# Expert rows gathered from token order and outputs scattered to token order through index lists made on chip, in place of sorted copies in DRAM

## The chip, the cores and the metric

One core of a Trainium2 chip runs the whole program. The metric is device time in microseconds (us); lower is better. TensorE is PE, VectorE is DVE, ScalarE is ACT, GpSimd is POOL and SyncE is SP. Everything is float32.

## The reference, cut to what matters

Two transformer blocks run one after the other on 512 tokens of 1024 features. The first has four recurrent mixers, a layer norm, a top-4-of-32 mixture of experts and a gated embedding; the second has two layers of retention, pooling and attention. The change touches the experts only:

```
logits = x2d @ router_w + router_b
top_val, top_idx = top_k(logits, 4);  gate = softmax(top_val)
# the 2048 assignments are sorted by expert into blocks of rows of one expert
hg, hl = split(xblk @ w_gu[e] + b_gu[e]);  hg = min(hg, 7);  hl = clip(hl, -7, 7)
y = (hg * sigmoid(1.702 * hg) * (hl + 1)) @ w_down[e] + b_down[e]
ffn[token] = sum over its four assignments of gate * y
```

## The kernel before, in words

**Stages.** The input projection with the four mixers fills the first 470 us, then come the output projection, the norm and the router (to about 549 us), then the experts (to about 1639 us), the sum over the four assignments with the gated embedding (to about 1700 us), and the second block.

**Blocks.** The 2048 assignments are laid out in blocks of 96 slots (3 groups of 32 lanes), each block of one expert, at most 56 blocks; slots that an expert does not fill stay empty. With these inputs the loop turns 32 times, one block for each expert, so on average 64 of the 96 slots hold a token. `dest` (L2993) is the slot of each assignment: 96 x block + 32 x group + lane.

**The sorted copies.** `x_sorted` and `y_sorted` are DRAM arrays with one row of 4 KB for each of the 5376 slots. SP fills both with zeros at the start (L1849 to L1858, 44 MB, in six transfers between the first weight pieces), and only then loads the masks into the place that the zeros came from (L1861). After the router, POOL scatters each token's row four times into `x_sorted` (L1959, 16 indirect transfers of 128 rows, 8 MB). ACT reads the rows of a block in four transfers of 32 partitions by 3 groups by 1 KB (`from_sorted`, L637 to L641), each slot's row being four quarters of 1 KB, and writes the outputs of a block in four more (L2265 to L2267). After the loop POOL gathers from `y_sorted` the four outputs of each token (L1967, 16 indirect transfers).

**One turn of the loop.** Every engine runs the same loop and meets the others at semaphores; `Turn` (L285) makes the values out of the turn's number. PE (L1376): gate_up(1), (2), (3), which are three quarters of this block's first product, then gate_up(0) and the bias of the next block, then the down product. A weight piece is 2 MB; a block takes six, kept in six ring slots that SP refills as PE frees them (L1901 to L1915). DVE (L3029): finds the next block's expert, waits for the next block's rows (`rows_landed`, L3056), transposes half of them aside, waits until PE is done with gate_up(1), transposes the other half into `xg` (L3059, counted in `rows_turned`), and only then adds the bias and clips for this block's groups (L3035 to L3038), which is what PE's next gate_up(0) waits for (`gu_drained`). ACT: at `rows_turned` it issues the load of the rows two blocks on, then the sigmoids, the bias copy, the three copies of the outputs out of PSUM (L2263), and their store.

**Around the loop.** The first block's rows do not come from DRAM: PE picks them out of SBUF with a one-hot product (L1351). The second block's rows are the first load (L2244); ACT waits for all 16 scatters before it (L2243). After the loop ACT waits for all stores, raises `all_stored`, and POOL gathers; DVE adds the weighted outputs tile by tile (L3075), in between normalizes the meta tokens, and PE follows with the gated embedding.

## Time and profile before

| | us |
|---|---|
| Median of 3 runs (3220.64 to 3222.08) | 3221.12 |
| The profiled execution's own time | 3224.01 |
| Its span, first to last instruction | 3221.9 |
| PE busy | 3060.8 (95%) |
| DVE busy | 1206.7 (37%) |
| ACT busy | 557.6 (17%) |
| POOL busy | 49.0 (2%) |
| Bytes moved by DMA | 743.71 MB |

The table is of one profiled execution. A busy PE is one that has matmuls in flight. The parts of the page and the answers of the trace say of each idle stretch what ended it, and of each transfer how long it took from its issue until it landed. The granted clock is PE's, as a share of full speed.

### The profile page before, as it was taken

To read this page: it belongs to the slowest core of one execution; us is meant where nothing else is said; L and a number is where in the kernel's file an instruction comes from. 1 tells how busy PE (TensorE), PEld (TensorE's weight loads), DVE (VectorE), ACT (ScalarE), POOL (GpSimd) and SP (SyncE) were. 2 spreads that over 40 slices of the span, in tenths; PEclk is the share of its full clock that TensorE was granted. 3 is DMA by queue.
4 is the path that set the end of the run, shared out by engine and by line. 5 is a ranking of instruction groups with operands and counts; after the bars stand their busy time and mean duration, and the time that the engine had idled before them with its cause. 6 is when DMAs were issued, how large, how long until landed. Compare 5 with 4: busy or idle time off the path is not lost.

```text
span 3221.9 us, 52861 instructions
## 1 busy us (share of the span) xinstructions
PE 3060.8 (95%) x22497; PEld 1727.1 (54%) x22497; DVE 1206.7 (37%) x2398; ACT 557.6 (17%) x1138; POOL 49.0 (2%) x58
## 2 busy tenths in 40 slices
PE   9878889799999999999989999999999999999999
PEld 3355555243334333333434767675686748775866
DVE  1633365223222232323256443335425362335231
ACT  1332321011111111111112131131101411131000
POOL 0000001000000000000020000000000000000000
PEclk9888969899999999999989999999999999999999
DMA  9900115899999999999972333243434344242542
GB/s 400 362 1 27 53 38 213 327 406 411 406 408 404 404 409 404 410 405 413 402 275 94 135 111 145 104 177 131 165 129 158 135 176 151 105 177 105 196 164 97
DMA packets 100924, 743.71 MB, mean 231 GB/s; under 512 B 11512, under 2 KB 38720, under 8 KB 57936
## 3 DMA queue, kind: packets, MB, share of 16 engines
q1 hardware_dynamic: 62224, 687.49, 53.8%
q10 hardware_dynamic: 32624, 30.52, 2.9%
q0 software_dynamic: 5968, 24.14, 1.9%
q8 instruction: 82, 1.34, 0.2%
q14 instruction: 26, 0.21, 0.0%
HBM read 674.98 MB, written 67.13 MB: 230 GB/s over the span
## 4 chain that ended last, share of the span: by engine, by line
PE 51%; DMA 29%; DVE 5%; issue 2%; ACTq 1%; ACT 1%; POOL 1%; DVEq 0%; SPq 0%
DMA arena<-x_sorted 28%; PE psum L1727 20%; PE psum L1704 11%; PE psum L1661 3%; PE psum L1650 3%; PE psum L899 1%; ACTq L641 1%; PE psum L1452 1%; PE psum L917 1%; PE psum L1293 1%; PE psum L1768 1%; PE psum L1416 1%; PE psum L1508 1%; DMA x_sorted<-arena 1%; PE psum L1554 1%
## 5 line engine op out<-in xcount | busy, mean ns | idle before, releaser
L1341 PE MATMUL psum<-weight_ring,arena 128*32 128x512 f32 x6192 | 676.0, 594 | 42.2 <-DVE arena L3035 41.5
L1727 PE MATMUL psum<-arena,weight_ring 128*128 128x256 f32 (+1 forms) x2816 | 638.5, 385 | 2.8 <-ACT arena L2380 2.8
L1727 PEld LDWEIGHTS psum<-arena,weight_ring 128*128 128x128 f32 x2816 | 530.0, 190 | 101.2 <-issue 12.9
L1341 PEld LDWEIGHTS psum<-weight_ring,arena 128*32 128x32 f32 x6192 | 199.9, 110 | 498.7 <-issue 455.8
L1416 PE MATMUL psum<-weight_ring,arena 128*32 128x256 f32 x6144 | 338.2, 380 | 0.0
L1416 PEld LDWEIGHTS psum<-weight_ring,arena 128*32 128x32 f32 x6144 | 196.7, 110 | 152.9 <-issue 26.8
L3057 DVE STREAM_TRANSPOSE arena<-arena 128x384 f32<-128x384 f32 x32 | 18.6, 580 | 643.1 <-DMA arena<-x_sorted 643.1
L1704 PE MATMUL psum<-weight_ring 128*128 128x512 f32 x468 | 204.1, 593 | 4.9 <-DMA weight_ring<-down 3.7
L1704 PE MATMUL psum<-weight_ring,arena 128*128 128x512 f32 x470 | 204.4, 593 | 0.7 <-ACT arena L2380 0.7
L3414 DVE TENSOR_TENSOR weight_ring<-weight_ring,psum 128x256 f32<-128x256 f32 (+1 forms) x88 | 37.4, 425 | 432.9 <-PE psum L1727 431.3
L3314 DVE TENSOR_TENSOR weight_ring<-weight_ring 128x1024 f32<-128x1024 f32 (+1 forms) x140 | 157.2, 1172 | 8.6 <-PE psum L1704 7.8
L1704 PEld LDWEIGHTS psum<-weight_ring 128*128 128x128 f32 x468 | 88.5, 190 | 116.0 <-issue 108.8
L1704 PEld LDWEIGHTS psum<-weight_ring,arena 128*128 128x128 f32 x470 | 89.0, 190 | 111.7 <-issue 109.9
L915 PE MATMUL psum<-arena,weight_ring 128*128 128x512 f32 x288 | 134.0, 616 | 11.1 <-DMA weight_ring<-weights 6.8
L2440 ACT ACTIVATE weight_ring<-psum 128x256 f32<-128x256 f32 (+1 forms) x88 | 34.1, 387 | 586.5 <-PE psum L1727 586.3
L1661 PE MATMUL psum<-arena,weight_ring 128*128 128x272 f32 (+1 forms) x512 | 116.8, 386 | 0.0
L2257 ACT ACT_TABLE_LOAD x32 | 41.1, 1283 | 417.0 <-issue 417.0
L1661 PEld LDWEIGHTS psum<-arena,weight_ring 128*128 128x128 f32 x512 | 96.1, 189 | 19.9 <-issue 2.8
L915 PEld LDWEIGHTS psum<-arena,weight_ring 128*128 128x128 f32 x288 | 54.6, 196 | 76.7 <-issue 67.3
L917 PE MATMUL psum<-weight_ring,arena 128*128 128x512 f32 (+1 forms) x192 | 90.9, 601 | 0.0
L2263 ACT COPY arena<-psum 128x256 f32<-128x256 f32 x96 | 36.0, 375 | 293.2 <-PE psum L1416 286.7
L1650 PE MATMUL psum<-weight_ring,arena 128*128 128x262 f32 (+2 forms) x320 | 86.2, 426 | 0.0
(446 smaller groups left out, 2716.3 us busy)
## 6 DMA issues: line engine op xcount, KB each, us to landing
weight_ring<-exp_gu SPq DMA_DIRECT2D x129, 2048.0 KB, 11.4
weight_ring<-weights SPq DMA_DIRECT2D x80, 2048.0 KB, 7.8
weight_ring<-exp_down SPq DMA_DIRECT2D x64, 2048.0 KB, 10.8
weight_ring<-down SPq DMA_DIRECT2D x48, 1024.0 KB, 6.1
x_sorted<-arena SPq DMA_DIRECT2D x2, 10752.0 KB
arena<-x_sorted ACTq DMA_DIRECT2D x132, 96.0 KB, 21.0
y_sorted<-arena ACTq DMA_DIRECT2D x128, 96.0 KB, 16.8
y_sorted<-arena SPq DMA_DIRECT2D x2, 5632.0 KB, 39.4
```

Source lines behind the costliest of these rows:

```text
L915: mm = pe.matmul(bank, w[:, k, a:a + P], x_t[:, k, :], start=(k == 0), stop=(k == KT - 1))
L917: mm = pe.matmul(bank[:, 0:width], x_t[:, k, t * P:(t + 1) * P], w[:, k, a:a + width], start=(k == 0), stop=(k == KT - 1))
L1341: mm = pe.matmul(psum[j * GROUP:(j + 1) * GROUP, g, :], xg[:, k // 4, g, k % 4 * GROUP:(k % 4 + 1) * GROUP], w[:, kk, j * 512:(j + 1) * 51 ...
L1416: mm = pe.matmul(psum[j * GROUP:(j + 1) * GROUP, 3 + g, 0:256], hid_t[:, g, k * GROUP:(k + 1) * GROUP], w[:, kk, j * 256:(j + 1) * 256], s ...
L1650: mm = pe.matmul(bank[:, 0:width], h2_t[:, k, OFF[t]:OFF[t] + P], w[:, k, 0:width], start=first, stop=last)
L1661: mm = pe.matmul(bank[:, 0:b - a], w[:, k, c:c + P], h2_t[:, k, a:b], start=first, stop=last)
L1704: mm = pe.matmul(bank, left[stationary][:, q, :], right[part][f][half][:, n, :], start=(q == 0 and name not in ADDED_TO), stop=(q == pairs ...
L1727: mm = pe.matmul(bank[:, 0:b - a], w[:, k, col:col + P], h2_t[:, k, a:b], start=(k == 0), stop=(k == KT - 1))
L2257: T.did(act.activation(sig[:, g, :], swi[:, g, 0:256], ACT.Sigmoid, scale=SWIGLU_ALPHA), swish_given)
L2263: T.did(act.copy(y_out[:, g, :], psum[:, 3 + g, 0:256]), y_drained)
L3314: V.did(dve.tensor_tensor(b[out[0]][out[1]], b[one[0]][one[1]], b[other[0]][other[1]], op), right_ready)
L3414: V.did(dve.tensor_tensor(g, g, bank[:, 0:b - a], ALU.mult), main.drained["v"])
```

## The change

The sorted copies go. `token_rows` holds the 512 normalized rows in token order, as 2048 quarters of 1 KB; `y_tokens` holds an output for each assignment, at row (choice, token, quarter). Every block's load becomes three indirect transfers on POOL's queue, one for each group, whose 128 partitions are 4 quarters by 32 lanes; every store becomes three indirect transfers likewise. The row numbers come from two lists, `idx_x` and `idx_y` (128 partitions by 168 group slots). They come out of a product: for each of the 16 (tile, choice) pairs a one-hot of the lane times the number of the assignment, against a one-hot of the group slot (64 matmuls of 128 x 32 against 128 x 168), and ten DVE instructions on the sum. A slot without a token gets a number beyond the bound, and the transfer is told to pass over such numbers. The zeros at the start go, the masks and the weight pieces are loaded without them, and the loads after the loop become four direct ones of 2 MB on SP's queue.

```diff
-CONST3 = Layout(before=P, iota=P, split=SPLITS, lane=1)
+SLOT_UNITS = NB * GROUPS
+UNIT_PARTS = (5, 11)
+STEP = 1024
+NOWHERE = 65536
+CONST3 = Layout(before=P, iota=SLOT_UNITS, split=SPLITS, lane=1, ids=TT * TOP, quarter=1)
...
-        x_sorted = nc.dram_tensor("x_sorted", (SORTED, D), F32, kind="Internal").ap()
-        y_sorted = nc.dram_tensor("y_sorted", (SORTED, D), F32, kind="Internal").ap()
+        token_rows = nc.dram_tensor("token_rows", (SEQ * 4, 256), F32, kind="Internal").ap()
+        y_tokens = nc.dram_tensor("y_tokens", (SEQ * TOP * 4, 256), F32, kind="Internal").ap()
...
                 gate_up(0, first_used)
+                pe.wait_ge(sem("first_rows_ready"), 2)
+                for n in range(TT * TOP):
+                    units = one_u[0][:, n, :] if n < UNIT_PARTS[0] else one_u[1][:, n - UNIT_PARTS[0], :]
+                    for j in range(4):
+                        mm = pe.matmul(psum[j * GROUP:(j + 1) * GROUP, SLOT_BANK, 0:SLOT_UNITS], one_r[:, n, :], units, start=(n == 0),
+                                       stop=(n == TT * TOP - 1), skip_group_check=True)
+                mm.then_inc(sem("rows_picked"), 1)
                 pe.wait_ge(rows_turned, 2)
...
-            sp.wait_ge(sem("zeros_ready"), 1)
-            store_zeros(x_rows, 0, SORTED // P // 2, sem("rows_stored"))
-            load_piece(2)
...
-            sp.wait_ge(sem("rows_stored"), 32)
-            sp.wait_ge(y_stored, 64)
             sp.dma_start(c1[:, P:P + D], io["const1"][:, P:P + D]).then_inc(sem("masks_landed"), 16)
-            for n in range(5, 9):
+            for n in range(2, 9):
                 load_piece(n)
...
             sp.wait_ge(sem("all_stored"), 1)
+            load_given(0)
             load_piece2(1, io["ple_gate"][1])
+            load_given(1)
+            load_given(2)
+            sp.wait_ge(sem("ffn_ready"), 1)
+            load_given(3)
...
         def _(pool):
-            pool.memset(zero_row, 0.0).then_inc(sem("zeros_ready"), 1)
-            pool.wait_ge(sem("rows_stored"), 32)
             for t in range(TT):
                 pool.wait_ge(sem("x1_ready"), t + 1)
                 pool.tensor_copy(x1_by_tile[:, t], x1[:, t, :].rearrange("p (q k j) -> p k q j", q=4, k=KT)
                                  ).then_inc(sem("x1_by_tile_ready"), 1)
-            pool.wait_ge(sem("dest_ready"), 1)
...
+                pool.dma_start(token_rows[t * P * 4:(t + 1) * P * 4, :].rearrange("(p q) d -> p (q d)", q=4), x1[:, t, :]
+                               ).then_inc(y_stored, 16)
+
+            def gather_rows(index):
+                for g in range(GROUPS):
+                    pool.indirect_dma_start(rows_in[:, g, :], None, token_rows, bass.IndirectOffsetOnAxis(ap=index[:, g:g + 1], axis=0),
+                                            bounds_check=SEQ * 4 - 1, oob_is_err=False).then_inc(rows_landed, 16)
+
+            pool.wait_ge(y_stored, 16 * TT)
+            pool.wait_ge(sem("rows_listed"), 1)
+            gather_rows(idx_x[:, GROUPS:2 * GROUPS])
...
+            with pool.Fori(0, blocks) as i:
+                T = Turn(pool, i, own, per, credit, sem("expert_pool_passed"))
+                T.wait(rows_turned, 1)
+                T.hold()
+                T.did(pool.tensor_copy(now_x, idx_x[:, bass.ds((i + 2) * GROUPS, GROUPS)]))
+                T.settle()
+                T.hold()
+                gather_rows(now_x)
+                T.wait(y_drained, GROUPS)
+                T.hold()
+                T.did(pool.tensor_copy(now_y, idx_y[:, bass.ds(i * GROUPS, GROUPS)]))
+                T.settle()
+                T.hold()
+                for g in range(GROUPS):
+                    pool.indirect_dma_start(y_tokens, bass.IndirectOffsetOnAxis(ap=now_y[:, g:g + 1], axis=0), y_out[:, g, :], None,
+                                            bounds_check=SEQ * TOP * 4 - 1, oob_is_err=False).then_inc(y_stored, 16)
+            pool.wait_ge(y_stored, blocks * BLOCK_DONE + 16 * TT)
+            pool.sem_inc(sem("all_stored"), 1)
...
-                act.wait_ge(sem("scattered"), 16 * TT * TOP)
-                from_sorted(act, slice(ROWS_B, 2 * ROWS_B), rows_landed)
...
-                    T.wait(rows_turned, 1)
-                    from_sorted(act, bass.ds((i + 2) * ROWS_B, ROWS_B), rows_landed)
...
-                    T.wait(y_drained, GROUPS)
-                    for j in range(4):
-                        dst = y_sorted[bass.ds(i * ROWS_B, ROWS_B), j * 256:(j + 1) * 256].rearrange("(g r) n -> r g n", g=GROUPS)
-                        act.dma_start(dst, y_out[j * GROUP:(j + 1) * GROUP, :, :]).then_inc(y_stored, 16)
...
-                V.did(dve.tensor_copy(dest, dest_f), sem("dest_ready"))
+                then(dve.tensor_copy(dest, dest_f))
+                V.did(dve.tensor_scalar(lane_i, dest, GROUP - 1, None, ALU.bitwise_and))
+                then(dve.tensor_scalar(unit_i, dest, 5, None, ALU.logical_shift_right))
+                V.did(dve.tensor_copy(lane_f, lane_i))
+                then(dve.tensor_copy(unit_f, unit_i))
...
+                then(dve.tensor_tensor(one_r, each_of(iota[:, 0:GROUP], pairs), along(lane_f, GROUP), ALU.is_equal))
+                V.did(dve.tensor_tensor(one_r, one_r, along(CONST3(c3, "ids"), GROUP), ALU.mult))
+                for part, at in enumerate((0, UNIT_PARTS[0])):
+                    of = unit_f[:, at:at + UNIT_PARTS[part]]
+                    V.did(dve.tensor_tensor(one_u[part], each_of(iota, UNIT_PARTS[part]), along(of, SLOT_UNITS), ALU.is_equal))
+                V.settle()
+                V.did(dve.memset(den, 0.0), sem("first_rows_ready"))
...
+                dve.wait_ge(sem("rows_picked"), 3)
...
+                then(dve.tensor_scalar(empty, token, 0.0, float(NOWHERE), ALU.is_equal, ALU.mult))
...
+                V.did(dve.tensor_copy(idx_x, empty))
...
+                V.did(dve.tensor_copy(idx_y, token), sem("rows_listed"))
```

## Rows read from the trace of the kernel before

**Rows 1.** Page, part 4: the chain that ended last, by line.

```profile
DMA arena<-x_sorted 28%; PE psum L1727 20%; PE psum L1704 11%; PE psum L1661 3%; PE psum L1650 3%; PE psum L899 1%; ACTq L641 1%; PE psum L1452 1%; PE psum L917 1%; PE psum L1293 1%; PE psum L1768 1%; PE psum L1416 1%; PE psum L1508 1%; DMA x_sorted<-arena 1%; PE psum L1554 1%
```

**Rows 2.** Windows: stretch, length, busy by engine, granted clock, DMA share, GB/s.

```profile
549.00:604.00 55.00, 29.96 (x255) 14.03 (x258) 10.10 (x23) 1.58 (x3) 17.03 (x16) 0.78 0.83 327
...
611.90:1627.90 1016.00, 998.22 (x12156) 387.24 (x12160) 283.34 (x776) 129.39 (x248) 0.00 (x0) 1.00 1.00 402
```

**Rows 3.** Waits in the loop: total us, times, longest.

```profile
DVE arena L3057 <- DMA arena<-x_sorted: 605.0, 30, 22.9
...
PE psum L1341 <- DVE arena L3035: 17.8, 15, 1.7
```

**Rows 4.** PE's timeline: start, length, work; first, two middle, last down product.

```profile
611.81 10.57 PE L1416 MATMUL psum<-weight_ring,arena 128*32 128x256 f32 x192
...
1004.26 10.57 PE L1416 MATMUL psum<-weight_ring,arena 128*32 128x256 f32 x192
1014.65 20.78 PE L1341 MATMUL psum<-weight_ring,arena 128*32 128x512 f32 x192
...
1036.35 10.57 PE L1416 MATMUL psum<-weight_ring,arena 128*32 128x256 f32 x192
...
1627.82 10.57 PE L1416 MATMUL psum<-weight_ring,arena 128*32 128x256 f32 x192
```

**Rows 5.** DMA queues, 612 to 1628 us: packets, MB, share of 16 engines.

```profile
q1 hardware_dynamic: 26359, 383.85, 93.0%
q10 hardware_dynamic: 27776, 24.40, 7.4%
```

**Rows 6.** Row loads: landing time in the loop, and for the first load.

```profile
DMA to landing us min/median/max: 2.2/21.8/31.7
...
arena<-x_sorted ACTq DMA_DIRECT2D x4, 96.0 KB, 2.4
```

**Rows 7.** PE's timeline between the router and the first down product.

```profile
545.91 10.65 PE L1351 MATMUL psum<-arena 128*128 128x96 f32 x64 [1.32 <-issue]
556.50 5.36 PE L1341 MATMUL psum<-weight_ring,arena 128*32 128x512 f32 x48
...
564.23 15.66 PE L1341 MATMUL psum<-weight_ring,arena 128*32 128x512 f32 x144 [0.71 <-issue]
...
603.61 7.27 PE L1341 MATMUL psum<-weight_ring,arena 128*32 128x512 f32 x48 [23.73 <-DVE arena L3035]
```

**Rows 8.** DVE's timeline in the same stretch.

```profile
547.62 0.69 DVE L2991 TENSOR_TENSOR arena<-arena 128x512 f32<-128x512 f32 x1
...
549.07 0.17 DVE L2993 CAST arena<-arena 128x16 int32<-128x16 f32 x1
...
549.22 2.01 DVE L2996 TENSOR_TENSOR arena<-arena 128x1792 f32<-128x1792 f32 x1
...
601.94 0.58 DVE L3057 STREAM_TRANSPOSE arena<-arena 128x384 f32<-128x384 f32 x1 [38.13 <-DMA arena<-x_sorted]
```

**Rows 9.** The chain over the wait for the 16 scatters.

```profile
570.20 27.86 DMA x_sorted<-arena
```

**Rows 10.** POOL: an indirect issue in the timeline; its copies' group, mean ns.

```profile
552.56 0.99 POOL L1959 DMA_INDIRECT x_sorted<-arena  x1 [0.30 <-issue]
...
L1953 POOL COPY arena<-arena 128x1024 f32<-128x1024 f32 x4 | 4.2, 1062 | 530.8 <-DVE arena L2937 530.8
```

**Rows 11.** Waits of PE in the first 200 us: total us, times, longest.

```profile
PE psum L915 <- DMA weight_ring<-weights: 6.8, 2, 6.2
```

**Rows 12.** After the loop: timelines of ACT, DVE, POOL; one SP issue.

```profile
1639.00 2.93 ACTq L2267 DMA_DIRECT2D y_sorted<-arena  x4
...
1656.71 3.93 DVE L3075 SCALAR_TENSOR_TENSOR arena<-weight_ring,arena 128x1024 f32<-128x1024 f32 x3 [3.08 <-DMA weight_ring<-y_sorted,arena]
...
1666.03 2.88 POOL L1967 DMA_INDIRECT weight_ring<-y_sorted,arena  x1 [0.30 <-issue]
...
weight_ring<-ple_gate SPq DMA_DIRECT2D x1, 2048.0 KB, 8.6
```

83 lines of the change are left out of this document (42 added, 41 removed).

## The prediction

> **What bounds the kernel now.** I read the chain that ended last first: its largest line, 28% of the span, is the transfer of block rows out of `x_sorted` [rows 1]. The windows say where that is: from the first to the last down product (1016 us) PE is busy for 998 us at the full granted clock, while the DMA engines are busy all the time at 402 GB/s; in the 55 us before, PE is busy for only 30 us [rows 2]. The waits then separate the two: DVE stands 605 us for block rows, but that costs PE only 17.8 us, in 15 turns, where the next gate_up finds its PSUM bank not drained [rows 3]. PE's timeline gives the floor: where nothing waits, a turn is 1036.35 - 1004.26 = 32.09 us of matmuls back to back, and the 31 turns between the first and the last down product took 1627.82 - 611.81 = 1016.0 us, or 32.77 us each [rows 4]. So the loop is held by PE, with 1016.0 - 31 x 32.09 = 21.2 us on top that come from late rows.
>
> Why are they late? The queue of the weights (q1) and that of row loads and stores (q10) carried almost the same number of packets, 26359 and 27776, but 383.85 against 24.40 MB [rows 5]. Four row transfers land 2.4 us after their issue when alone, but 21.8 us (median) and up to 31.7 us in the loop [rows 6]. I read this as turns taken between the queues: a 1 KB packet waits for a 16 KB one. Per turn of the loop the engines spend 0.930 x 1016 / 31 = 30.5 us on weights and 0.074 x 1016 / 31 = 2.4 us on rows, 32.9 us in all. They are as full as PE is.
>
> **The change, part by part.**
>
> *Zeros, 44 MB, gone.* They share the queue with the weight pieces, but in the first 200 us PE waits for weights only 6.8 us, of which 6.2 us are the very first pieces, ahead of any zero [rows 11]. What hides the zeros is that a piece is asked for one piece ahead of its use. Nothing gained; nothing can be lost, since queue and SP only get emptier. The masks land earlier than before, for users that did not wait. Price 0.
>
> *Scatters gone, start of the loop.* Now POOL scatters 16 times, the chain stands 27.86 us behind the last of them [rows 9], DVE gets the second block's rows at 601.94 us [rows 8], and PE resumes at 603.61 us after an idle time of 23.73 us [rows 7]. After the change:
> - DVE builds one-hots behind `dest` (549.07 us): two of 512 elements at 0.69, one of 840 and one of 1848 at 2.01 for 1792, which is 0.9 and 2.1, and five small ones at 0.17 and the gaps between them, some 1.2 [rows 8]: 5.6 us. All that DVE makes next (`routed`, gates) is 5.6 us later, which SP and POOL wait for; the one-hots are ready at about 555 us, while PE still picks the first rows and runs gate_up(0) until 556.50 + 5.36 = 561.9 us [rows 7].
> - PE: 64 products are 128 instructions. Nearest in the shape of the weights are the down products, 10.57 / 192 = 0.055 us each [rows 4]: 7.0 us. The picking of rows, with full 128 x 128 weights, gives the upper bound, 10.65 / 64 = 0.166 us [rows 7], or 21 us; 168 columns against 256 would give 4.6 us. I take 7.0: PE is done at 568.9 us.
> - DVE makes the lists: ten instructions of 168 columns between 0.17 and 0.69 us [rows 8]; I take 0.25 each, 2.5 us: `rows_listed` at 571.4 us. ACT and POOL wait for it.
> - POOL: three indirect issues at 0.99 and 0.3 apart [rows 10], 3.6 us, up to 575.0. The four direct ones that write `token_rows` before, each behind a copy of 1.06 us [rows 10], cost no more than an indirect one and lie between tiles of the norm that come 7 to 9 us apart. The rows land 2.4 us after the last issue if alone, 31.7 us at most [rows 6]. Few weights are under way then (the next piece is asked for when gate_up(1) ends), so I take 2.4 to 12 us: 577 to 587 us.
> - PE meanwhile: the bias (564.23 - 561.86 = 2.4 us with its waits) and three pieces, 15.66 us [rows 7], so 568.9 + 2.4 + 15.7 = 587.0 us against 603.61. Then one piece and the bias take 5.4 + 0.9 us (1036.35 less the end of 1014.65 + 20.78) where 603.61 to 611.81 were 8.2 us [rows 4, 7]. Gain 16.6 + 1.9 = 18.5 us; I take 18. With products at 0.166 us only 4 would be left; with rows 31.7 us in flight, about 603 + 1 us, nothing.
>
> *The loop.* Slots without a token are passed over: 64 rows instead of 96, times four quarters, and again for the stores. If such a slot leaves no packet behind, rows cost 2/3 of 2.4 = 1.6 us of the engines, 32.1 us in all: no more than PE's 32.09. And the turns taken drop from 768 data packets to 512, so two thirds of 31.7 us, about 21 us, for a load that has a whole turn of 32.09 us. Ahead of it are POOL's copy of three words (0.1 to 1.06 us) and three issues, 3.6 us [rows 10]: 21 + 4.7 + DVE's 1.2 us for two transposes of 0.58 [rows 8] = 27 us, under 32.09. POOL's wait for `y_drained` has only the store and then the next load behind it, which comes later anyway; ACT, freed of eight issues, was not late. So every turn takes 32.09 us: gain 21.2 us, which is also all that there is. If a passed slot still takes its turn in the queue, the queue is as full as before and the gain is 0.
>
> POOL's issues may be slower than 0.99 us: one of its gathers took 2.88 us beside DVE's instructions of 1.3 us [rows 12]. At 2.88 for each of three, a load would be ready 1.2 + 1.1 + 9.5 + 21 = 32.8 us after the one before, which is today's turn and would take back the loop's gain; but DVE's block-sized instructions there are like its transposes, 0.58 us [rows 8], half of 1.3. I take 0.99. Of the rules on the chip this is where one speaks against the change: the page SBUF — State Buffer of the Trainium skill (SBUF: two separate sides) says that descriptors of transfers issued on GpSimd are not written while DVE holds the port pair that the two share. The row of 2.88 us agrees with it.
>
> *After the loop.* Now the last copy is followed by ACT's issue at 1639.0 us, POOL's gathers and DVE's start at 1656.71 us after 3.08 us of waiting [rows 12]. After: POOL's copy and three scatters, 4.1 us, landing in about 2.4 us [rows 6], then 2 MB by SP; such a load took 8.6 us [rows 12]. 1639.0 + 4.1 + 2.4 + 8.6 = 1654.1 us, so DVE starts 2.6 us earlier, and at best 3.1, because its down bias ends then. The other three loads, 5 us each at 402 GB/s, keep ahead of DVE's four instructions of 1.3 us and the norm of the meta tokens. With 2.88 us an issue it would be 6 us later: bounds -3 and +3.1. I take 2.6.
>
> **Sum.** 18 + 21.2 + 2.6 = 41.8 us, off an execution of 3224.0 us (a span of 3221.9 and 2.1 around it), so 3182.2; that execution was 2.9 us above the median of the runs, so against the median 3221.1 - 41.8 = 3179.3. I say 3179.
>
> **Rivals.**
> 1. *The loop gains nothing* (passed slots still take their turns, or the row queue is as full as before). For it: I have no row of an indirect transfer that passes anything over. Against: two fewer semaphore rounds a block. Only start and end count, 20.6 us: 3200. Chance 0.17.
> 2. *The products for the lists are slow or the first gather is late*: start 0 to 4 us instead of 18, the loop as forecast: 3193 to 3197. For it: 0.166 us per matmul in the row next to it. Chance 0.07.
> 3. *Slower: the gather on POOL's queue becomes the cycle.* Place: from `rows_turned` to the next `rows_landed`. If all 96 slots keep their turns and the flight stays 31.7 us after the last issue, it is 1.2 + 31.7 + 0.5 for POOL's copy + 3.6 = 37.0 us a turn: (37.0 - 32.77) x 31 = 131 us lost, less 20.6: 3332. With 2.88 us for each issue [rows 12] it is 43 us. It decides from a turn of 32.77 + 20.6 / 31 = 33.4 us on. Against it: in that flight the earlier issues already move, so issue time is not simply added, and passed slots shorten it. The State Buffer page's lock would act at this place. Chance 0.06.
>
> The forecast has 0.70. **The numbers.** 3179, at best 3177 (PE's floor, DVE's 3.1 us, 19 us at the start); low 3173 for what I mis-timed at the start. The upper end takes in rivals 1 and 2: 3205. A measurement can tell about 0.2%, 6.4 us. Slower by more than that: rival 3, 0.06. Within: 0.02, a part of rivals 1 and 3. Faster: 0.92.
>
> **What would show it.** Right: down products 32.09 us apart in all turns, no PE wait on L3035 in the loop, DVE's wait for rows ended well before the bank is filled; fewer than 512 + 96 packets a turn on POOL's queue; PE resumes near 587 us without a wait; DVE starts its sums 2 to 3 us after its down bias at most. Wrong: turns of 33 us or more ended by row transfers (rivals 1 and 3), a PE row for the list products well above 7 us (rival 2), PE idle on weights, or a first 549 us that is not what it was.

## The result, and the profile after

The changed kernel takes 3163.7 us (median of 4 runs, 3162.7 to 3164.6) against 3221.2 us: a ratio of 0.9824, interval 0.9808 to 0.9841. That is 57.5 us less where 41.8 were forecast, 15.7 us more, and below the range of 3173 to 3205. The profiled execution took 3164.56 us, its span is 3162.7 us. One execution further down, the profiled one of rows_by_act_3k, ran at a granted clock of 0.65 from end to end (4541.5 us) and is left out of every comparison.

The chain that ended last no longer holds the row transfer that led it [rows 1]. The page of the changed kernel, parts 1, 3 and 4 (columns as in the table ahead of the change):

```profile
PE 3049.8 (96%) x22625; PEld 1725.8 (55%) x22625; DVE 1218.2 (39%) x2417; ACT 559.4 (18%) x1138; POOL 225.7 (7%) x288
...
HBM read 675.00 MB, written 16.80 MB: 219 GB/s over the span
...
PE 84%; DVE 4%; ACT 2%; issue 1%; DMA 0%; DVEq 0%; SPq 0%; ACTq 0%
```

PE's timeline, from the picking of the first rows to the first three down products, the last one, and the first product of the second block:

```profile
541.01 9.37 PE L1360 MATMUL psum<-arena 128*128 128x96 f32 x64 [1.33 <-issue]
550.31 5.36 PE L1350 MATMUL psum<-weight_ring,arena 128*32 128x512 f32 x48
555.48 4.78 PE L1383 MATMUL psum<-arena 128*32 128x168 f32 x128
560.19 1.06 PE L1338 MATMUL psum<-arena 32*32 32x512 f32 x8
561.18 20.81 PE L1350 MATMUL psum<-weight_ring,arena 128*32 128x512 f32 x192
581.92 1.06 PE L1338 MATMUL psum<-arena 32*32 32x512 f32 x8
582.91 10.57 PE L1432 MATMUL psum<-weight_ring,arena 128*32 128x256 f32 x192
...
1577.67 10.57 PE L1432 MATMUL psum<-weight_ring,arena 128*32 128x256 f32 x192
```

PE waits for nothing any more between the picking and the last down product, against 23.73 us of idleness in [rows 7] and 17.8 us in [rows 3]. The 31 turns take 1577.67 - 582.91 = 994.8 us, which is 31 x 32.09.

Windows of the start and of the loop, columns as in [rows 2]; then waits of DVE and the queues in the loop (583 to 1577 us):

```profile
541.00:582.90 41.90, 41.89 (x448) 21.29 (x448) 27.19 (x65) 4.11 (x7) 6.33 (x7) 0.95 0.58 213
582.90:1577.60 994.70, 994.70 (x12156) 389.40 (x12152) 286.80 (x777) 131.47 (x248) 200.37 (x248) 1.00 0.99 403
```

```profile
DVE arena L3105 <- PE psum L1350: 457.5, 31, 14.9
...
DVE arena L3103 <- DMA arena<-token_rows,arena: 3.6, 1, 3.6
...
q1 hardware_dynamic: 26409, 384.46, 94.4%
q0 software_dynamic: 9037, 15.97, 4.2%
...
y_tokens<-arena POOLq DMA_INDIRECT x93, 7.1
arena<-token_rows,arena POOLq DMA_INDIRECT x93, 7.5
```

DVE, which stood 605 us for rows [rows 3], now waits for PE instead; rows are 7.5 us in flight for 21.8 [rows 6]. POOL's queue carries 9037 / 31 = 292 packets a turn for the 896 of [rows 5]. Some 96 of them are packets of 4 bytes, 16 for each of the six transfers, which I take for those that raise its semaphore; of those that hold rows most hold 4 KB, four quarters at once.

Both programs were profiled a second time, on other chips (picking starts on L1351 and L1360; the stretches are the same for both):

| us | before | before_again | after | after_again |
|---|---|---|---|---|
| span | 3221.9 | 3209.5 | 3162.7 | 3167.6 |
| until picking starts | 545.9 | 537.8 | 541.0 | 543.2 |
| picking to first down product | 65.9 | 65.9 | 41.9 | 43.2 |
| 31 turns | 1016.0 | 1019.1 | 994.8 | 994.8 |
| last down product to second block | 116.7 | 114.3 | 112.7 | 114.2 |
| second block | 1477.4 | 1472.5 | 1472.4 | 1472.3 |

So the three stages that the change touches give 24.0, 21.2 and 4.0 us in the first pair and 22.7, 24.4 and 0.1 us in the second, 49.2 and 47.2 together. The other 9.9 us of the first pair lie in stretches without an edit. The time until picking starts does not depend on which of the two kernels a run is made from: over the 19 profiles used here it lies between 537.0 and 546.3 us, with runs of both near either end (before 545.9 and before_by_group 537.8; act_3k_strided 546.3 and pool_by_group 537.0).

### The profile page after: what moved, and what is told of

Read it like the earlier page. It is cut to its first block, busy times and chain, and to the rows that moved or that the text cites. A ratio compares the mean times of both kernels' runs of the same rounds, so it can differ in the third digit from the quotient of the medians.

```text
span 3162.7 us, 53140 instructions
## 1 busy us (share of the span) xinstructions
PE 3049.8 (96%) x22625; PEld 1725.8 (55%) x22625; DVE 1218.2 (39%) x2417; ACT 559.4 (18%) x1138; POOL 225.7 (7%) x288
## 4 chain that ended last, share of the span: by engine, by line
PE 84%; DVE 4%; ACT 2%; issue 1%; DMA 0%; DVEq 0%; SPq 0%; ACTq 0%
PE psum L1350 21%; PE psum L1743 20%; PE psum L1720 11%; PE psum L1432 11%; PE psum L1677 3%; PE psum L1666 3%; PE psum L908 1%; PE psum L1468 1%; PE psum L1302 1%; PE psum L926 1%; PE psum L1784 1%; PE psum L1338 1%; PE psum L1524 1%; PE psum L1570 1%; PE psum L1453 1%; PE psum L1598 1%
## 5 line engine op out<-in xcount | busy, mean ns | idle before, releaser
L1432 PEld LDWEIGHTS psum<-weight_ring,arena 128*32 128x32 f32 x6144 | 196.9, 110 | 152.7 <-issue 26.8
L3081 DVE TENSOR_TENSOR arena<-psum,arena 128x512 f32<-128x512 f32 x96 | 65.1, 678 | 210.2 <-PE psum L1350 210.2
L2277 ACT ACTIVATE arena<-arena 128x256 f32<-128x256 f32 x96 | 40.1, 417 | 468.8 <-DVE arena L3083 468.8
L1965 POOL DMA_INDIRECT arena<-token_rows,arena x99 | 101.1, 1021 | 80.1 <-DVE arena L3073 31.9
L1989 POOL DMA_INDIRECT y_tokens<-arena x96 | 97.0, 1011 | 49.7 <-POOL arena L1985 28.3
## 6 DMA issues: line engine op xcount, KB each, us to landing
weight_ring<-forget_rows ACTq DMA_DIRECT2D x12, 264.0 KB, 10.1
```

Source lines behind the costliest of these rows:

```text
L1432: mm = pe.matmul(psum[j * GROUP:(j + 1) * GROUP, 3 + g, 0:256], hid_t[:, g, k * GROUP:(k + 1) * GROUP], w[:, kk, j * 256:(j + 1) * 256], s ...
L1965: pool.indirect_dma_start(rows_in[:, g, :], None, token_rows, bass.IndirectOffsetOnAxis(ap=index[:, g:g + 1], axis=0), bounds_check=SEQ * ...
L1989: pool.indirect_dma_start(y_tokens, bass.IndirectOffsetOnAxis(ap=now_y[:, g:g + 1], axis=0), y_out[:, g, :], None, bounds_check=SEQ * TOP ...
L2277: T.did(act.activation(sig[:, g, :], swi[:, g, 0:256], ACT.Sigmoid, scale=SWIGLU_ALPHA), swish_given)
L3081: T.did(dve.tensor_tensor(swi[:, g, :], psum[:, g, :], b_gu, ALU.add), gu_drained)
```

## The experiments

All are timed beside the kernel before, whose median was 3210 to 3219 us on these chips, so ratios are more apt than differences to 3221. "Turns" is the time between the first and the last down product; 994.8 us is PE's floor. Packets, landing times and GB/s are of the stretch from 615 to 1560 us. Where all 96 slots move, the bytes of a turn are the same in every run, so that GB/s states the length of a turn once more and is no second evidence for it.

### Do the zeros count, do the scatters, do the passed slots?

**zeros_back**: the 44 MB of zeros are stored again, the masks behind them.

```diff
+            store_zeros(x_rows, 0, SORTED // P // 2, sem("rows_stored"))
+            load_piece(2)
...
+            sp.wait_ge(sem("rows_stored"), 96)
             sp.dma_start(c1[:, P:P + D], io["const1"][:, P:P + D]).then_inc(sem("masks_landed"), 16)
```

> The changed kernel, with the 44 MB of zeros stored again where they were, into arrays that nobody reads, and the masks loaded behind them. Theory A (the zeros never cost anything; the 4.9 us by which the changed kernel reaches its row picking earlier come from another granted clock in the mixers): the time stays at 3163.7 within 3 us, and the milestones up to 200 us do not move. Theory B (the zeros delayed the mixers): picking starts at 545 to 546 us again and the time is 3168 to 3170.

3166.9 us (3162.7 to 3169.8), ratio 0.9842 (0.9826 to 0.9859). Windows of the first 200 us, with the zeros and (second line) in the changed kernel:

```profile
0.00:200.00 200.00, 170.16 (x757) 81.30 (x757) 75.14 (x111) 56.48 (x89) 1.16 (x5) 0.94 0.77 307
```

```profile
0.00:200.00 200.00, 169.69 (x756) 81.46 (x756) 74.39 (x110) 55.75 (x86) 0.20 (x4) 0.95 0.23 87
```

The DMA engines move 307 instead of 87 GB/s and PE is as busy. The zeros cost nothing.

**scatters_back**: the 16 scatters stand in front of the first gather again.

```diff
+            pool.wait_ge(sem("first_rows_ready"), 2)
+            for t in range(TT):
+                for n in range(TOP):
+                    at = TOP * t + n
+                    pool.indirect_dma_start(x_sorted, bass.IndirectOffsetOnAxis(ap=dest[:, at:at + 1], axis=0),
+                                            x1[:, t, :], None).then_inc(sem("scattered"), 16)
+            pool.wait_ge(sem("scattered"), 16 * TT * TOP)
             pool.wait_ge(y_stored, 16 * TT)
```

> The changed kernel, with the 16 scatters of 8 MB made again on POOL's queue after the router, into an array that nobody reads, and waited for before the first gather. Theory A (the wait for the scatters was the start's price): the first down product comes 20 to 27 us later, DVE waits for rows some 20 to 30 us there, and the time is 3184 to 3191, the upper end if the second block loses its better granted clock with it. Theory B (most of the start's gain was a better clock and PE's shorter products, not the wait): less than 12 us, up to 3175.

3196.6 us (3194.5 to 3199.1), ratio 0.9933 (0.9916 to 0.9949): some 30 us are back, a few more than expected. Its timelines of POOL, then PE:

```profile
598.91 1.06 POOL L1966 DMA_INDIRECT arena<-token_rows,arena  x1 [27.54 <-DMA x_sorted<-arena]
```

```profile
605.39 7.73 PE L1351 MATMUL psum<-weight_ring,arena 128*32 128x512 f32 x48 [21.93 <-DVE arena L3089]
```

This is the stall of [rows 7] and [rows 9] again; the first down product starts at 614.0 for 582.9 us. It is longer than what the change took away because the scatters now stand behind the one-hots: the last of them is issued 570.4 - 541.1 = 29.3 us after the picking starts, for 570.2 - 545.9 = 24.3 us in the kernel before. The turns stay at 994.8 us. So the start belongs to the scatters, and the loop's gain to something else.

**all_slots**: empty slots load some valid row and store to places of their own, so that all 96 rows of a block move, in and out, 768 quarters of 1 KB a turn.

```diff
-                then(dve.tensor_scalar(empty, token, 0.0, float(NOWHERE), ALU.is_equal, ALU.mult))
...
+                then(dve.scalar_tensor_tensor(slots, empty, float(DUMP), slots, ALU.mult, ALU.add))
...
+                then(dve.tensor_scalar(row, empty, lane, None, ALU.mult))
```

> The changed kernel, with every slot moved: a slot without a token loads some valid row and stores into a row of its own beyond the outputs, so 768 data packets a turn on POOL's queue in place of 512; eight or so more DVE instructions of 168 columns before the loop. Theory A (passed slots leave no packet behind, and that is what frees the queue): turns of 32.8 us and more again, PE waits of some 20 us in the loop, 3180 to 3190. Theory B (the queue of the rows has room for all 96 slots when POOL issues them in this order): turns stay at 32.09 us, only the start is 2 to 3 us later, 3164 to 3168. Rival 3 of the prediction (the cycle through POOL binds once the slots are all moved): 3280 or more.

3165.5 us (3163.5 to 3167.8), ratio 0.9833 (0.9816 to 0.9849), turns 994.8 us. Its queues and landing times:

```profile
q1 hardware_dynamic: 25497, 371.35, 94.6%
q0 software_dynamic: 8356, 22.82, 6.1%
...
y_tokens<-arena POOLq DMA_INDIRECT x87, 7.0
arena<-token_rows,arena POOLq DMA_INDIRECT x87, 7.6
```

Half as many bytes again, the same number of packets, the same landing time: what I gave as the reason for the loop's gain, the slots passed over, is not the reason.

### Is it the queue, or the number of packets?

I took packets as the next theory. In the changed kernel the loop's loads and stores were replaced by plain transfers of all 96 slots. Each of the four loads of a turn fills the 32 neighbouring partitions of one quarter, as before the change. The loads take 96 fixed rows of `token_rows`, and after the loop 2048 fixed rows are summed.

**rows_by_act_1k**: on ACT's queue, in runs of 1 KB. **rows_by_act_3k**: the same, but a partition's three groups are one run of 3 KB. **rows_by_pool_direct**: the runs of 1 KB, issued by POOL.

```diff
+            for q in range(4):
+                src = rows[0:ROWS_B, q * 256:(q + 1) * 256].rearrange("(g r) n -> r g n", g=GROUPS)
+                engine.dma_start(rows_in[q * GROUP:(q + 1) * GROUP, :, :], src).then_inc(rows_landed, 16)
...
+                    T.wait(rows_turned, 1)
+                    load_rows(act)
```

> The changed kernel, but the loop's row loads and stores go back to ACT's queue, in four transfers each of runs of 1 KB (96 rows of a fixed place of token_rows in place of the gathered ones, outputs stored by slot; the loads after the loop read the first 2048 of those rows). Start stage, lists and the loads after the loop stay. Theory A (packets: 768 of 1 KB and 128 semaphore packets a turn take turns one for one with 16 KB weight packets): about 896 packets a turn on ACT's queue, landing about 20 us after issue, turns above 32.09 us again in about half of the turns, PE waits on the bias and clip about 18 us in all, the loop's gain of 21 us gone: 3164 + 21 = 3185 us. Rival (something else of the change freed the loop: earlier one-hots, an emptier start, ACT freed of issues before the loop): turns 32.09 us, 3164 to 3167 us.

> As the one before, still on ACT's queue with the same bytes and the same number of transfers, but each partition's three groups are one run of 3 KB in DRAM, for loads and stores. Theory A (number of packets): about 256 data and 128 semaphore packets a turn, landing 8 to 11 us after issue, all turns 32.09 us, no PE wait on the bias: 3164 us (3162 to 3167). Rival B (the queue or the engine that issues is what made the rows late, whatever their packets): as the 1 KB form, about 3185 us, landing near 20 us.

> As rows_by_act_1k, the same runs of 1 KB, but the four loads and four stores of a turn are issued by POOL as plain transfers. Theory C (POOL's queue packs four runs of 1 KB into a packet, whatever the transfer): 192 data packets a turn, landing 6 to 9 us after issue, turns 32.09 us: 3164 us (3162 to 3167). Theory D (only indirect transfers are packed): 768 data packets a turn, landing about 20 us or more, and PE waits again: 3185 us or somewhat more.

rows_by_act_1k took 3197.0 us (3193.3 to 3205.7), ratio 0.9938 (0.9921 to 0.9955), turns 1018.9 us: the old loop is back, and the time is 12 us above the 3185 expected (the profiled execution, whose loop this is, was the fastest at 3193.3 us). rows_by_act_3k took 3177 to 3186 us; its loop is read from rows_by_act_3k_2, the same kernel (below). rows_by_pool_direct took 3190.6 us (3188.5 to 3191.2), ratio 0.9908 (0.9892 to 0.9925), turns 1020.1 us. The waits of PE, queues and landings of rows_by_act_1k, then of rows_by_pool_direct:

```profile
PE psum L1361 <- DVE arena L3069: 19.2, 18, 1.6
...
q1 hardware_dynamic: 24762, 360.62, 94.0%
q10 hardware_dynamic: 25534, 22.43, 7.3%
...
weight_ring<-exp_gu SPq DMA_DIRECT2D x114, 2048.0 KB, 11.9
...
arena<-token_rows ACTq DMA_DIRECT2D x112, 96.0 KB, 23.6
```

```profile
PE psum L1361 <- DMA weight_ring<-exp_gu: 10.2, 19, 0.6
...
q1 hardware_dynamic: 24454, 356.20, 94.2%
q0 software_dynamic: 10977, 22.52, 6.7%
...
weight_ring<-exp_gu SPq DMA_DIRECT2D x114, 2048.0 KB, 26.8
...
arena<-token_rows POOLq DMA_DIRECT2D x116, 96.0 KB, 11.4
```

On POOL's queue the runs are packed here too (no packet of 1 KB; 4096 and 2048 bytes in the packet records) and rows are in time. But now the weights are late: the first nine turns take 32.09 us, the others some 33.2. The same bytes went through at 417 GB/s in all_slots and go at 401 here. Something of the transfers' form costs the loop 3 to 4% of its rate, whether it then shows as late rows or as late weights.

### Place in DRAM, form, or queue?

**before_again** and **after_again** are the two kernels unchanged; their rows stand in the table above. **indirect_in_order** is the changed kernel with lists that name neighbouring rows in DRAM. **direct_spread** is rows_by_pool_direct with rows that lie apart in DRAM; after its loop rows of `token_rows` are summed.

```diff
+                V.did(dve.tensor_copy(idx_x, token))
+                then(dve.tensor_scalar(empty, empty, 1.0, None, ALU.add))
+                then(dve.tensor_scalar(token, empty, 4.0, CONST3(c3, "quarter"), ALU.mult, ALU.add))
...
-                src = rows[0:ROWS_B, q * 256:(q + 1) * 256].rearrange("(g r) n -> r g n", g=GROUPS)
+                src = rows[0:5 * ROWS_B, q * 256:(q + 1) * 256].rearrange("(g r k) n -> k r g n", g=GROUPS, k=5)[0]
```

> The kernel before, unchanged, for a second profile. Open: the first 541 us of the changed kernel were 4.9 us shorter and its second block 5.0 us shorter, both where the granted clock differed, with no edit there. If the clock's levels there vary from execution to execution: picking starts anywhere between 541 and 546 us and the second block takes 1472 to 1478 us, unlike the first profile. If they belong to the program: 545.9 us and 1477.4 us again, within 0.5 us. Time 3215 to 3222 us either way.

> The changed kernel, unchanged, on a further chip beside the kernel before. In the second profile of the kernel before, picking began 8.1 us earlier (537.8 for 545.9 us) and the second block took 1472.5 for 1477.4 us: levels of the granted clock in stretches without an edit. If the change itself is worth what its three stages show (start 24.0, loop 21.2 to 24.4, after the loop 1.6 to 4.0, together 47 to 52 us) and the rest of the 57.5 us was the clock of the first pair: 3167 to 3172 us beside 3219. If the whole 57.5 us belongs to the change: 3162 us or less. Turns 32.09 us all the way and no PE wait in the loop in either case.

> The changed kernel, but its lists name the places of the kernel before: every block's load reads 96 neighbouring rows of token_rows (modulo 512) and its outputs go to the 96 neighbouring rows of the block, with all slots moved. Open from rows_by_pool_direct: why its turns were 33.3 us with weights late, though its bytes a turn are those of all_slots, whose turns were 32.09 us. Theory P (place: 384 KB of neighbouring rows slow the DMA engines, weights with them): turns about 33.3 us, PE waits on weight pieces, landing of weights above 20 us, 16 KB packets 655 ns in the mean, 3190 us. Theory F (form: plain transfers of 32 partitions, 256 data packets a turn for 192): as all_slots, turns 32.09 us, 630 ns, 3164 to 3168 us.

> As rows_by_pool_direct, the same eight plain transfers on POOL's queue, but the 96 rows of a load lie 5 rows apart in token_rows, and those of a store 56 rows apart; the loads after the loop read token_rows. Theory P (place): turns 32.09 us, no late weights, 3164 to 3168 us. Theory F (form): turns about 33.3 us from some 320 us into the loop on, 3190 us.

> The same kernel as rows_by_act_3k, whose profiled execution ran at a granted clock of 0.65 throughout and says nothing of the balance in the loop; its other four took 3177 to 3186 us. Theory A (packets alone): rows land in 8 to 12 us, no PE wait on the bias and clip; 3164 us if nothing else binds. From the four times I expect instead that rows are no longer late but weights are, as in rows_by_pool_direct: turns of 32.6 to 33.0 us ended by weight pieces, landing of weights above 20 us, 3177 to 3186 us. Theory B (the queue, whatever its packets): waits on the bias and clip near 19 us, rows landing near 20 us.

before_again: 3217.9 us, ratio 0.9998 (0.9982 to 1.0014). after_again: 3166.4 us (3162.9 to 3169.5), ratio 0.9851 (0.9819 to 0.9883). indirect_in_order: 3168.5 us (3163.3 to 3172.1), ratio 0.9856 (0.9824 to 0.9888), turns 994.8 us. direct_spread: 3195.5 us (3186.7 to 3203.3), ratio 0.9949 (0.9928 to 0.9970), turns 1014.2 us. rows_by_act_3k_2: 3184.8 us (3181.9 to 3189.3), ratio 0.9914 (0.9881 to 0.9946), turns 1013.7 us. DMA lines of the last three in this order:

```profile
DMA packets 33902, 394.19 MB, mean 417 GB/s; under 512 B 5640, under 2 KB 5640, under 8 KB 11245
```

```profile
DMA packets 35644, 380.45 MB, mean 403 GB/s; under 512 B 6427, under 2 KB 6427, under 8 KB 13809
```

```profile
PE psum L1361 <- DMA weight_ring<-exp_gu: 13.8, 18, 1.0
...
q1 hardware_dynamic: 24618, 358.54, 94.1%
q10 hardware_dynamic: 11111, 22.79, 6.8%
```

Neither another place in DRAM (1014.2 for 1020.1 us) nor another queue (1013.7 us on ACT's, 1020.1 on POOL's) frees the loop, and packets of 3 KB instead of 1 KB turn late rows into late weights without bringing the turns back to 994.8 us. What is left is the form.

### The 32 neighbouring partitions

**pool_strided** is rows_by_pool_direct in all but one thing: a transfer's 32 partitions are every fourth one. **act_1k_strided** and **act_3k_strided** do the same to the two forms on ACT's queue; **loads_strided** and **stores_strided** do it to rows_by_act_1k for the loads or the stores alone. The features of a row come to lie elsewhere.

```diff
-                engine.dma_start(rows_in[q * GROUP:(q + 1) * GROUP, :, :], src).then_inc(rows_landed, 16)
+                engine.dma_start(rows_in[q:P:4, :, :], src).then_inc(rows_landed, 16)
...
-                engine.dma_start(dst, y_out[q * GROUP:(q + 1) * GROUP, :, :]).then_inc(y_stored, 16)
+                engine.dma_start(dst, y_out[q:P:4, :, :]).then_inc(y_stored, 16)
```

**pool_by_group** and **before_by_group** move a group in one plain transfer over 128 partitions, the one in rows_by_pool_direct, the other in the kernel before (the lines are the latter's):

```diff
+                src = rows[g * GROUP:(g + 1) * GROUP, :].rearrange("r (q n) -> q r n", q=4)
+                engine.dma_start(rows_in[:, g, :], src).then_inc(landed, 16)
```

> As rows_by_pool_direct in all, its eight transfers of 32 partitions by three runs of 1 KB too, but the 32 partitions of a transfer are every fourth one in place of 32 neighbours (the features of a row come to lie elsewhere, so the outputs mean nothing). Theory N (neighbours: SBUF's partitions of one quarter are what slows the engines): turns 32.09 us, weights landing near 10.5 us, 3164 to 3169 us. Theory K (packets: 4096 and 2048 bytes, 256 data and 128 semaphore packets a turn): turns near 33.2 us, 3186 to 3196 us.

> As rows_by_pool_direct (plain transfers on POOL's queue, neighbouring rows in DRAM), but three loads and three stores a turn, one for each group, over all 128 partitions by 1 KB, which is the shape of the changed kernel's indirect transfers. Theory S (shape: transfers of 32 partitions by 3 KB use up more of the DMA engines than 128 by 1 KB, whatever addresses them): 192 data packets of 4 KB a turn, all turns 32.09 us, 417 GB/s, weights landing near 10.5 us, 3164 to 3169 us. Theory I (being indirect is what matters): turns near 33.2 us with weights late, 3186 to 3196 us.

> The kernel before, its row loads and stores still on ACT's queue in runs of 1 KB, but by group, 3 + 3 transfers of 128 partitions by 1 KB, in place of 4 + 4 of 32 by 3 KB. If the number of 1 KB packets is what makes rows late (768 data packets either way): rows land some 20 us after issue, PE waits for the bias and clip 15 to 20 us in all, 3205 to 3220 us. If the shape alone made the old loop late: landing under 12 us, turns 32.09 us, 24 us less than the kernel before: about 3192 us.

> As rows_by_act_1k (ACT's queue, 768 packets of 1 KB a turn, which gave turns of 32.87 us and rows 23.6 us in flight), but each transfer's 32 partitions are every fourth one. Theory Q (two causes: the count of packets makes rows late, the neighbouring partitions slow every packet): the 16 KB packets fall from 644 to about 635 ns, but rows still land some 19 to 23 us after issue, so PE still waits on bias and clip, 10 to 19 us: 3175 to 3190 us. Theory N alone (rows were late only because the engines were slowed and full): landing well under 15 us, turns 32.09 us, 3164 to 3168 us.

> As rows_by_act_3k (ACT's queue, 256 packets of 3 KB a turn, turns of 33.2 us bound by weights), but each transfer's 32 partitions are every fourth one. Theory N (neighbouring partitions slow the engines): turns 32.09 us, weights landing near 10.5 us, 417 GB/s, 3164 to 3168 us. If it were POOL's queue that needs the spread places and ACT's not: 3182 to 3189 us as before.

> As rows_by_act_1k, but only the loads of rows go to every fourth partition; the stores still read 32 neighbours. Theory W (it is the writing of SBUF that slows the engines, which write the weights there too): turns 32.09 us, 3164 to 3170 us. Theory R (the reading for the stores does it): as rows_by_act_1k, turns 32.8 to 32.9 us, 3185 to 3197 us. If both carry a part, between: 16 KB packets above 630 ns in the mean and some turns above 32.09 us.

> As rows_by_act_1k, but only the stores read every fourth partition; the loads still write 32 neighbours. Theory W: as rows_by_act_1k, 3185 to 3197 us, turns 32.8 to 32.9 us. Theory R: turns 32.09 us, 3164 to 3170 us.

| | turns, us | GB/s | rows in flight | weights (gate_up) landing | median, us | ratio (interval) |
|---|---|---|---|---|---|---|
| POOL, 32 neighbours | 1020.1 | 401 | 11.4 | 26.8 | 3190.6 | 0.9908 (0.9892, 0.9925) |
| POOL, every fourth | 994.8 | 417 | 8.7 | 10.8 | 3164.3 | 0.9831 (0.9799, 0.9862) |
| ACT 3 KB, 32 neighbours | 1013.7 | 404 | 11.7 | 26.6 | 3184.8 | 0.9914 (0.9881, 0.9946) |
| ACT 3 KB, every fourth | 994.8 | 417 | 9.3 | 10.6 | 3170.0 | 0.9844 (0.9817, 0.9871) |
| ACT 1 KB, 32 neighbours | 1018.9 | 405 | 23.6 | 11.9 | 3197.0 | 0.9938 (0.9921, 0.9955) |
| ACT 1 KB, every fourth | 994.8 | 417 | 16.6 | 10.0 | 3167.7 | 0.9842 (0.9815, 0.9868) |
| ACT 1 KB, loads every fourth | 996.1 | 416 | 14.5 | 10.1 | 3172.0 | 0.9868 (0.9832, 0.9904) |
| ACT 1 KB, stores every fourth | 1019.7 | 406 | 19.8 | 11.6 | 3192.7 | 0.9933 (0.9911, 0.9955) |

The queues and landings of act_1k_strided, to be held against rows_by_act_1k above, and PE's only wait in loads_strided beside that of stores_strided:

```profile
q1 hardware_dynamic: 25467, 370.91, 94.0%
q10 hardware_dynamic: 26306, 23.10, 7.1%
...
weight_ring<-exp_gu SPq DMA_DIRECT2D x117, 2048.0 KB, 10.0
...
arena<-token_rows ACTq DMA_DIRECT2D x116, 96.0 KB, 16.6
```

```profile
PE psum L1361 <- DVE arena L3069: 0.9, 1, 0.9
```

```profile
PE psum L1361 <- DVE arena L3069: 19.7, 20, 1.6
```

ACT's queue carries as many packets of 1 KB a turn as ever, about as many as the weights' queue has in all, and the loop runs at PE's floor. The share of q1 is the same 94.0%, but it now moves 25467 instead of 24762 packets in the same 945 us: 0.940 x 945 x 16 / 25467 = 0.558 us each on average for 0.574. (As the share is the same, this too only restates the shorter turn.) In each of the three pairs of the table only the partitions differ, and its last two lines tell the loads from the stores: with the loads alone spread PE waits once, 0.9 us (the time, 3172.0 us, is a little above the 3164 to 3170 expected); with the stores alone it waits as before. The late rows of the kernel before come from loads that write 32 neighbouring partitions. The forecast of act_1k_strided by two causes (3175 to 3190 us) was wrong, that by one cause alone right, except that rows are 16.6 us in flight and not under 15: the number of packets does lengthen a row's flight (16.6 us for 9.3 in 3 KB form), only not so far that it binds.

The two runs by group failed at their question. pool_by_group took 3268.3 us (ratio 1.0151, 1.0118 to 1.0185), before_by_group 3567.1 us (1.1081, 1.1044 to 1.1118), with turns of 35.4 and 44.0 us. The likely reason is the order in which the transfer is written down, quarters outermost; no run changes that order alone. ACT's timeline in one turn of before_by_group, DVE's and PE's behind it, and the DMA line:

```profile
889.38 20.66 ACTq L642 DMA_DIRECT2D arena<-x_sorted  x3
...
911.43 0.72 ACT L2258 ACTIVATE arena<-arena 128x256 f32<-128x256 f32 x2
911.88 0.43 DVE L3045 TENSOR_TENSOR arena<-arena 128x256 f32<-128x256 f32 x1 [13.46 <-ACT arena L2258]
...
914.05 3.21 PE L1342 MATMUL psum<-weight_ring,arena 128*32 128x512 f32 x16 [11.77 <-DVE arena L3037]
```

```profile
DMA packets 35279, 286.09 MB, mean 303 GB/s; under 512 B 2556, under 2 KB 18835, under 8 KB 18835
```

ACT stands 20.66 us in three issues that took 1.8 us for four before, so the sigmoids behind them are late and PE with them. Of the 2556 smallest packets 508 are of ACT's queue (16787 packets, of which 18835 - 2556 = 16279 hold 1 KB), some 4 for each of its 132 row transfers, where the form of the kernel before has 16. The Trainium skill (DMA: Bandwidth & Descriptors, section "Why a DMA increments its semaphore by 16 and not by 1") says that a transfer uses as many of the 16 DMA engines as the largest number up to 16 that divides the outermost dimension of both its sides; 4 on one side and 128 on the other give 4, and the count of 4 agrees. In pool_by_group each transfer shows 112 small packets ((20326 - 161 x 16) / 159), 16 for the semaphore and 96 more of 16 bytes; how many engines carry its data the records do not say. So neither run compares an indirect with a plain transfer of the same form; pool_strided does that.

## Why the prediction was right or wrong

**The failed step of the mechanism: "And the turns taken drop from 768 data packets to 512".** Size and place of the loop's gain were right, 21.2 us forecast and 21.2 measured (24.4 in the second pair), 32.09 us in every turn, no wait on the bias and clip. The reason was wrong, so that this agreement is luck. Passed slots do not lower the number of packets (all_slots), and fewer packets are not what makes the loop run free (act_1k_strided). The sign named ahead, fewer than 512 + 96 packets a turn, came true with 292, but because POOL's queue puts four quarters into a packet, not because slots are passed over.

Behind it stands a reading of mine, "They are as full as PE is": I took the busy share of the DMA engines, 30.5 + 2.4 us a turn at 402 GB/s, for what the bytes cost them. The share tells no such thing. Windows of the loop in the changed kernel, in all_slots and in rows_by_pool_direct (columns as in [rows 2]):

```profile
615.00:1560.00 945.00, 945.00 (x11604) 371.90 (x11604) 268.74 (x727) 125.97 (x237) 189.39 (x235) 1.00 1.00 408
```

```profile
615.00:1560.00 945.00, 945.00 (x11600) 372.35 (x11596) 271.42 (x736) 124.69 (x236) 187.36 (x232) 1.00 1.01 417
```

```profile
615.00:1560.00 945.00, 926.75 (x11272) 405.63 (x11268) 262.66 (x706) 121.56 (x229) 125.72 (x232) 1.00 1.01 401
```

The share is 1.00 to 1.01 whether PE is held up (the last) or not, and 408 or 417 GB/s go through without a wait where 401 or 402 did not suffice. 402 GB/s was what the engines did while part of their packets went to 32 neighbouring partitions. How much more than 417 they could do no run here shows.

No view of the kernel before shows a rate with the partitions spread while the loop runs, so the profile alone could not tell. The Trainium skill could have pointed there: SBUF — State Buffer, section "Door 1: The DMA port swizzle", says that DMA reaches SBUF through 16 ports, that four neighbouring partitions share one, and that partitions 0 to 31 reach only 8 of the 16. By its table every fourth partition reaches all 16. The runs agree as to what is slow and what is cured; that the ports are the cause is argued from the page, no run here names them. An indirect transfer whose rows all went to neighbouring partitions was not tried, so that being indirect counts for nothing rests on plain transfers reaching the same loop.

**The failed steps of the sum: the start, 18 for 24.0 us, and everything outside the change, put at nothing.** The three terms were forecast at 41.8 us together and measured 49.2 in the first pair; with 9.9 us outside them the time fell below the range.

**Start: 18 forecast, 24.0 and 22.7 measured; the largest mis-sized term of the change.** The list product took 4.78 us for the 7.0 taken; 168 for 256 columns had given 4.6, and should have been taken. Bias and its waits took 1.0 for 2.4 us, probably because the list product now covers the wait ahead of it. Picking took 9.37 for 10.65 us in the first pair, at a granted clock of 0.77 for 0.67 (10.62 us at 0.68 in after_again), so that 1.3 us of the 24.0 are not the change's. Rows landed long before PE came to them, as forecast. scatters_back confirms the stall itself: POOL goes on 28.5 us after it issued the last scatter, for 27.86 in [rows 9]. One bound was added up wrongly: a first gather 31.7 us in flight after POOL's last issue lands at 575.0 + 31.7 = 606.7 us, which would have lost 4 to 5 us and not "nothing"; it did not arise.

**After the loop: 2.6 forecast, 4.0 and 0.1 measured.** DVE starts its sums 24.68 us after the last down product for 28.89 before, 4.2 us earlier and more than the 3.1 called the best, because PE's product for the down bias ahead of them took 11.10 us at a granted clock of 0.64 for 12.64 at 0.55. The transfer chain is no longer what DVE waits for (0.40 us for 3.08 in [rows 12]). In the second pair DVE starts 26.3 us after the last down product for 28.9, 2.6 earlier. Part of it is lost again: in the norm of the meta tokens, between the sums, DVE waits 2.0 us for ACT in both profiles of the changed kernel, for 0.5 and 1.0 us before. From the first sum to the second block it is 88.0 and 87.9 us after the change, 87.8 and 85.4 before; why before_again is 2.4 us shorter there stays open.

**POOL's issues.** 0.99 us taken; 1021 and 1011 ns in the mean of 99 and 96. The longest of the loads in the loop took 1.06 us, so the lock that the prediction takes from the Trainium skill (SBUF — State Buffer, section "SBUF: two separate sides") and the 2.88 us of [rows 12] do not show there.

**Zeros.** Nothing forecast, nothing measured: zeros_back took 3166.9 us beside 3165.5 of all_slots on the same chip.

**What no step held: 9.9 us outside the change.** Until picking starts the two profiles of the kernel before differ by 8.1 us, more than either differs from the changed kernel, and its second block took 1477.4 and 1472.5 us. Among the 19 profiles the first is near the long end for the one stretch (537.0 to 546.3 us) and the longest for the other (1472.2 to 1473.8 us in the remaining 18). Where the second block begins the granted clock was 0.89 in the first profile and 1.00 in the second (16 us each), and from 200 to 300 us behind that 0.97 and 1.00. The first of these, before and before_again:

```profile
1744.00:1760.00 16.00, 15.53 (x153) 8.89 (x154) 14.25 (x17) 4.68 (x13) 6.45 (x12) 0.89 0.50 158
```

```profile
1737.00:1753.00 16.00, 15.98 (x157) 9.03 (x158) 14.78 (x18) 4.73 (x12) 6.44 (x12) 1.00 0.44 151
```

So by the stages of these two pairs 47 to 49 us of the 57.5 are the change's and the rest is the pair of executions. The medians leave more room: beside after_again the gain was 45.0 us, beside zeros_back 52.1, and the profile of before_again is the fastest of its ten executions (3211.7 for a median of 3217.9 us). The range's lower end allowed for mistimings at the start alone, not for clock levels outside the change. Why the times of the first chip differ so evenly over all its runs stays open.

**Rivals.** Rival 1's condition came true (the passed slots take their turns) and its price did not follow. Rival 2 fell with the 4.78 us product. Rival 3 needed a flight of 31.7 us; it was 7.5.

No version is faster than the changed kernel: from picking to the last down product PE has no idle time left. The same loop can be had without indirect transfers if loads reach all quarters of SBUF at once, but for the kernel before that means another layout of features over partitions; that was not built.

## What to carry to other kernels

Where the DMA engines are busy all the time, their rate is not a constant: look at which partitions each small transfer touches, and spread the loads over all of SBUF, before counting packets. Their busy share does not tell either: it was 1.00 or 1.01 with and without waits. Where rows and weights share full engines, a better packet form only changes which of them is late; the test is whether the turns get shorter. And a gain that comes as forecast is no proof of its reason: here the reason fell to the first run that put it alone.

## What the runs showed that I had not expected

- Eight small transfers a turn, 6% of the bytes, held all 16 engines together at 401 to 406 GB/s; with loads on every fourth partition it was 416 to 417. The loads (writing SBUF) do it, not the stores.
- POOL's queue packs rows of 1 KB: 768 of them make 192 data packets in indirect transfers of 128 rows and 256 in plain ones of 32 partitions. ACT's queue made one packet for each run, 1 KB or 3 KB.
- Slots passed over leave the number of packets as it is (288 a turn with and without them); where all four rows of a packet are passed over, the packet records show 16 bytes in its place.
- A plain load on ACT's queue written with a dimension of 4 outermost raised its semaphore with some 4 small packets for 16 and held ACT for 20.66 us in three issues.
- The DMA engines' busy share stood at 1.00 to 1.01 in loops of 401, 408 and 417 GB/s, with and without waits of PE.
